# Retention gates of a decoder step: the first and the last eighth of a block in two halves of the token columns

## What is computed

```
q, k, v, gate = split(rms(x) @ w_in)          # 4 heads, dk 256, dv 512
o, s_fin      = retention(rope(q), rope(k), v, s0)
o             = (o - mean(o)) * rsqrt(var(o) + eps)
x            += (silu(gate) * o) @ w_out
s_new[b]      = g^4 * s0[b] + k_b^T v_b       # sampled sequences b = 0..7, state 256 x 512 for each head
```

## Time and profile before

| what | value |
|---|---|
| median of 3 runs | 1598.01 us (1594.16 to 1599.3) |
| the profiled execution, own time | 1594.63 us |
| its span in the profile | 1592.8 us |
| PE matmul busy | 1524.2 us, 96% |
| DVE busy | 949.0 us, 60% |
| ACT busy | 550.5 us, 35% |
| stage of the gates, head 0 | 92.09 to 126.52 us |

### The profile page before, as it was taken

How to read it: one execution, slowest core, us unless ns; L and a number is a source line. 1 busy time by engine, 2 the same in 40 slices (tenths; PEclk the granted TensorE clock), 3 DMA queues, 4 the chain that set the end, 5 groups by cost and what they waited for, 6 DMA issues and landing times.

```text
span 1592.8 us, 27562 instructions
## 1 busy us (share of the span) xinstructions
PE 1524.2 (96%) x11425; PEld 1427.9 (90%) x11425; DVE 949.0 (60%) x1286; ACT 550.5 (35%) x853; POOL 123.5 (8%) x111
## 2 busy tenths in 40 slices
PE   7999999999999899999999999988789999999997
PEld 7779978978987799999999999887689999999997
DVE  6547437435634688547736667564558854763763
ACT  5233133123223353322322354353435332322331
POOL 0000001001000120000000021341221000000001
PEclk9999999999999999999999999898899999999999
DMA  6346217216323223123222242111112213223123
GB/s 236 113 164 218 93 61 264 93 60 209 135 80 119 107 93 106 66 93 106 79 93 93 79 150 70 60 41 54 41 39 82 106 66 111 88 79 119 67 79 109
DMA packets 50152, 164.05 MB, mean 103 GB/s; under 512 B 5264, under 2 KB 6608, under 8 KB 50032
## 3 DMA queue, kind: packets, MB, share of 16 engines
q1 hardware_dynamic: 41888, 134.56, 24.3%
q0 software_dynamic: 6416, 24.93, 4.3%
q10 hardware_dynamic: 1760, 3.31, 0.6%
HBM read 141.35 MB, written 23.46 MB: 103 GB/s over the span
## 4 chain that ended last, share of the span: by engine, by line
PE 84%; DVE 8%; issue 3%; ACT 3%; POOL 1%; ACTq 0%; DVEq 0%; POOLq 0%
PE ps L466 48%; PE ps L1127 13%; PE ps L480 8%; DVE arena L1406 3%; PE ps L1316 3%; PE ps L984 2%; PE ps L993 1%; DVE w_lo L454 1%; PE ps L1015 1%; PE ps L1001 1%; PE ps L1279 1%; PE ps L1307 1%; DVE rstd L515 1%; PE ps L971 1%; PE ps L1030 1%
## 5 line engine op out<-in xcount | busy, mean ns | idle before, releaser
L449 ACT ACTIVATE w_hi<-w_raw 128x1024 fp32r<-128x1024 f32 x180 | 188.7, 1055 | 383.5 <-PE ps L466 233.0
L466 PE MATMUL ps<-xg_hi,w_hi 128*128 128x272 f32 x1280 | 268.6, 291 | 14.1 <-DVE xg_lo L1412 7.8
L466 PE MATMUL ps<-xg_hi,w_lo 128*128 128x272 f32 x1280 | 265.3, 289 | 0.0
L466 PE MATMUL ps<-xg_lo,w_hi 128*128 128x272 f32 x1280 | 264.9, 288 | 0.0
L454 DVE TENSOR_TENSOR w_lo<-w_raw,w_hi 128x1024 fp32r<-128x1024 f32 x172 | 212.9, 1241 | 70.8 <-ACT w_hi L449 69.6
L466 PEld LDWEIGHTS ps<-xg_hi,w_hi 128*128 128x128 f32 x1280 | 203.1, 189 | 23.6 <-issue 12.7
L466 PE MATMUL ps<-pr_hi,w_hi 128*128 128x272 f32 x992 | 210.4, 291 | 8.2 <-DVE pr_lo L1406 4.5
L466 PE MATMUL ps<-pr_hi,w_lo 128*128 128x272 f32 x992 | 209.7, 290 | 0.0
L466 PE MATMUL ps<-pr_lo,w_hi 128*128 128x272 f32 x992 | 208.9, 290 | 0.0
L466 PEld LDWEIGHTS ps<-xg_lo,w_hi 128*128 128x128 f32 x1280 | 202.0, 189 | 0.0
L466 PEld LDWEIGHTS ps<-xg_hi,w_lo 128*128 128x128 f32 x1280 | 200.8, 189 | 0.0
(11 more groups left out here) (247 smaller groups left out, 2639.4 us busy)
## 6 DMA issues: line engine op xcount, KB each, us to landing
w_raw<-in_w SPq DMA_DIRECT2D x180, 512.0 KB, 3.5
arena<-in_w SPq DMA_DIRECT2D x40, 512.0 KB, 4.5
arena<-in_state SPq DMA_DIRECT2D x32, 512.0 KB, 4.8
out_st_s<-arena POOLq DMA_DIRECT2D x32, 512.0 KB, 4.3
x<-in_x ACTq DMA_DIRECT2D x4, 544.0 KB, 6.0
out_y<-x POOLq DMA_DIRECT2D x8, 272.0 KB, 2.3
out_st_p<-arena SPq DMA_DIRECT2D x4, 512.0 KB, 2.8
arena<-in_dec POOLq DMA_DIRECT2D x4, 256.0 KB, 2.9
```

Source lines behind the costliest of these rows:

```text
L449: nc.scalar.activation(w_hi[:, n.c % 4, :], w_raw[:, n.c % 2, :], ACT.Copy).then_inc(w_hi_done, 1)
L466: last = pe.matmul(ps[:, 2 * bank_pair + s, 0:HT], w_of(w, k), xm[:, k, s * HT:(s + 1) * HT], start=(k == 0 and w == 0 and xi == 0), stop= ...
```

## The change

A gate block's eight steps over k are issued by hand. In step 0 and in step 7 the three matmuls of the first half of the columns (bank 0) come first and then the three of the second half (bank 1); steps 1 to 6 alternate between the halves as before. When the first half's last matmul is done it raises a new semaphore, `gate_half`; the second half's last raises `blocks` as before. DVE copies each half by itself, 128x272, the first after `gate_half`, the second after `blocks`, and each raises `gate_pre`, which so counts 8 for a head in place of 4. PE's next block waits for the first copy ahead of its first-half matmuls and for the second copy ahead of its second-half matmuls. ACT's Silu and the later waits ask for both halves.

```diff
-                    act.wait_ge(gate_pre, (one.times(4) + (g + 1)).v)
+                    act.wait_ge(gate_pre, (one.times(8) + (2 * g + 2)).v)
...
+                def gate_part(g, k, halves):
+                    for w, xs in ((w_hi, xg), (w_lo, xg[:1])):
+                        for xi, xm in enumerate(xs):
+                            for s in halves:
+                                last = pe.matmul(ps[:, 2 * GATE_PAIR + s, 0:HT], w[:, g, k * P:(k + 1) * P], xm[:, k, halves_of(s)],
+                                                 start=(k == 0 and w is w_hi and xi == 0), stop=(k == KT - 1 and w is w_lo))
+                    return last
+
+                def gate(g):
+
+                    for s in range(2):
+                        if g:
+                            pe.wait_ge(gate_pre, (one.times(8) + (2 * g - 1 + s)).v)
+                        gate_part(g, 0, (s,))
+                    for k in range(1, KT - 1):
+                        if k == KT // 2:
+                            beside_gate(g)
+                        gate_part(g, k, (0, 1))
+                    gate_part(g, KT - 1, (0,)).then_inc(gate_half, 1)
+                    gate_part(g, KT - 1, (1,)).then_inc(blocks, 1)
+
                 pe.wait_ge(vlo_done, (one + 1).v)
                 for g in range(4):
                     pe.wait_ge(w_lo_done, (n + (4 + g + 1)).v)
-                    if g:
-                        pe.wait_ge(gate_pre, (one.times(4) + g).v)
-                    product(pe, GATE_PAIR, w_tile(Index(g)), KT, xg,
-                            lambda k: beside_gate(g) if k == KT // 2 else None).then_inc(blocks, 1)
+                    gate(g)
                     state(2 * g + 1)
...
                     new_state(2 * g)
+                    dve.wait_ge(gate_half, (one.times(4) + (g + 1)).v)
+                    tt(gate_t[:, g, 0:HT], ps[:, 2 * GATE_PAIR, 0:HT], rstd[:, 0:HT], ALU.mult).then_inc(gate_pre, 1)
                     dve.wait_ge(blocks, (n + (4 + g + 1 + BIAS)).v)
-                    tt(two(gate_t[:, g, :]), pair(GATE_PAIR), two(rstd[:, :]), ALU.mult).then_inc(gate_pre, 1)
+                    tt(gate_t[:, g, HT:T], ps[:, 2 * GATE_PAIR + 1, 0:HT], rstd[:, HT:T], ALU.mult).then_inc(gate_pre, 1)
                     new_state(2 * g + 1)
```

More of the change, by code:

```diff
@@ L259, in build @@
         upd_done, s_new, s_out = sem("upd_done"), sem("s_new"), [sem(f"s_out{s}") for s in range(S_SLOTS)]
-        cross_evac, so_done, gate_pre, gate_act, gate_kept = sem("cross_evac"), sem("so_done"), sem("gate_pre"), sem("gate_act"), sem("gate_kept")
+        cross_evac, so_done, gate_half, gate_pre, gate_act, gate_kept = sem("cross_evac"), sem("so_done"), sem("gate_half"), sem("gate_pre"), sem("gate_act"), sem("gate_kept")
         so_centred, so_sqrt, so_normed, so_turned = sem("so_centred"), sem("so_sqrt"), sem("so_normed"), sem("so_turned")
@@ L1056, in before @@
                     if c == 2:
-                        pe.wait_ge(gate_pre, (one.times(4) + 4).v)
+                        pe.wait_ge(gate_pre, (one.times(8) + 8).v)
                 def beside(c, k):
```

## The result

The changed kernel takes 1587.63 us as the median of 12 runs, the kernel before 1596.15 us as the median of its 12 runs; the ratio is 0.9948, with a 95% interval of 0.994 to 0.9957. That is 8.3 us faster (6.9 to 9.6). The forecast was 1592.0, with a range of 1587.5 to 1597.0: the time lies at the fast end of it, next to the 1588.9 of the rival in which the loads keep up, to which I had given 12 in 100. The gain forecast was 4.5 us.

What follows compares the result with a forecast made beforehand. PE was taken to bound the kernel, stopping twelve times for gate copies. Heads 0 to 2 gave 2.5 us, head 3 2.0: 4.5 us off the 1596.5 mean, forecast 1592.0 us, range 1587.5 to 1597.0.

Steps and rivals of the forecast that it cites:

- the rival in which the loads keep up: State 7's load lands 2 us earlier as POOL's write gets shorter; all is won, 7.6 us, 1588.9 us; 12 in 100.
- The stops: PE's twelve waits for gate-block copies, 0.67 us each: 0.05 stays, 0.62 won at each, 7.4 us for twelve.
- The costs: Matmul order costs nothing; two half copies add 0.15 us of DVE per block, 2.4 us, hidden by DVE's wait.
- The stall at cross_of(1): In gate block 2, heads 0 to 2, PE newly waits about 1.0 us for state 7's load; none in head 3.
- if nothing else changes the load lands 0.2 earlier: State 7's load, heads 0 to 2: new_state(1) starts 0.2 us earlier, then write 5.8 us and load 4.5 us.
- the bounds: State 7's load landing: 0.3 us later if state 2's write takes transfer share, 0.5 earlier if the weight block clears.
- The term of 0.2 + 0.62: Gain in each of heads 0 to 2: 0.2 us from two stops ahead of cross_of(1), 0.62 from the third.
- signs of being wrong: PE still waiting for copies, no gap at cross_of(1), state 1's write far from 5.8 us, or single-half matmuls over 0.126 us apart.
- The sum: Heads 0 to 2 give 2.5 us, head 3 gives 2.0; together 4.5 us, ends 2.3 and 5.7.
- low end of 2.3: Smallest summed gain, if 0.13 us stays of each stop and state 7's load is 0.3 later.
- the last head's 0.15: In the last head, DVE's new_state(7) and what follows, for which PE waits, start some 0.15 us sooner.

Runs made afterwards that it cites:

- the order alone: Kernel before with only PE's first and last eighth done half by half; DVE copies the whole block, PE waits once: 1596.81 us, ratio 1.0005.
- the swap: SP issues the first weight block ahead of state 6's load: 1586.07 us on the changed kernel, 1594.19 us on the kernel before.
- the first eighth: Changed kernel, but the last eighth alternates as before and both copies start after the block's end; PE waits half by half: 1595.49 us, ratio 0.9989.
- POOL's delay: Changed kernel, but POOL zeroes 8 unused columns ahead of each write of state 1 (also called the late write): 1594.59 us, ratio 0.9988.

## Why the forecast was right, and where it was not

**The stops.** Right, and a little low. 0.05 of each was to stay; the rows after show 3.50 against 3.48, so 0.02, and 0.65 won where I had 0.62. In heads 1 to 3 that is 1.93 to 1.96 for three stops.

**The costs.** Right. The order costs nothing (run of the order alone: 1596.81 us, ratio 1.0005). Two copies of 442 ns take 0.82 us from start to end because the second overlaps the first, so DVE's extra is 0.1 us for a block, and PE nowhere waits for a gate's copy any more. DVE's idle time, 0.61 us ahead of the first copy of gate 0 in head 0, covered it; DVE's busy time went from 949.0 to 951.6 us, and that did not decide the time here.

**The stall at cross_of(1).** The place was right: it is the load of state 7, over new_state(1) and the write of state 1, that PE meets there once the stops are gone, and head 0 showed it in both profiles of the change. new_state(1) starts 0.50 us after the block's end, not 0.67, much as forecast. The step that failed is "if nothing else changes the load lands 0.2 earlier". The write did not keep its 5.8 us. It took 4.2, 4.1 and 4.1 in heads 0 to 2, 1.5 to 1.6 us less; with the earlier start that is more than the 1.24 by which PE now comes sooner. Counted from the start of the stage, the load landed 0.7, 1.9 and 1.6 us earlier, where the bounds went from 0.3 later to 0.5 earlier. In heads 1 and 2 it was there in time, and in head 0, where it took 5.5 us and not 4.5, the wait was 0.6 and not 1.0. The term of 0.2 + 0.62 for each of these heads measured 1.38, 1.95 and 1.93. Two of the prediction's own signs of being wrong were there: a write of state 1 far from 5.8 us, and no gap in two of the three heads. What makes the load of state 7 take 3.9 us in one head and 6.5 in another of these eleven profiles stays open.

That is the rival in which the loads keep up, and its reason, that POOL's write starts sooner and has the transfers to itself for longer, was tested: over the seven profiled kernels with SP's old order there are 21 writes of state 1 in heads 0 to 2. Where the write was issued 0.23 to 0.35 us ahead of state 6's load, ten times, it took 5.0 to 5.9 us; where 0.46 to 0.84, eleven times, 4.0 to 4.6. The weight block, the other load beside the write, does not sort them: it came 1.16 to 1.45 us behind the write in both groups. In the four kernels with the swap the lead is 1.5 to 1.8 and the write takes 3.5 to 4.0. One POOL instruction that cut the lead brought the long writes and the waits back in two heads, and the swap took the long writes away again. I had bounded this trip with the write's 5.8 as a fixed term, though head 3 stood there with 3.7, and I read that as a write with less company. It had the same company: state 6's load and the weight block were issued 0.97 and 1.45 us behind it, in head 0 0.31 and 1.45. The change's 0.2 us were just the difference that a lead of 0.3 lacked. Why the write's time falls by over a us between a lead of 0.35 and one of 0.46 was not tested.

**The sum.** 7.0 us by the traces' stretches, 8.3 (6.9 to 9.6) by the runs. That is nearly twice the 4.5 that was forecast, and close to the 7.6 of the rival. The time lay inside the range because the range reached to that rival; my own sum was off in all of heads 0 to 2. Its low end of 2.3 also leaves out the last head's 0.15, which the high end has; that decides nothing.

The spans of the two profiled executions differ by 8.7. Up to the first matmul of the first SwiGLU layer's mixed products the changed kernel is 5.9 us ahead: the 7.0, less 0.65 by which the gates of head 0 begin later and 0.44 behind the retention layer. From that matmul to the same one of the second SwiGLU layer, where the change does nothing, it is 633.0 us before and 630.1 after, but also 630.5 in the run of the order alone and 634.1 in that of the first eighth, which has the change's copies; the change, run again, has 632.6. The stretch holds the window attention, where PE stands still at times and the granted clock falls for a while: in the kernel before PE is busy for 0.93 of the four us from 992, and in the next four its clock is 0.50. Four us of it in the kernel before, by windows (window, length; busy us of PE, PEld, DVE, ACT and POOL, each with its number of instructions; PE's granted clock; DMA share and GB/s):

```profile
1008.00:1012.00 4.00, 4.00 (x42) 3.08 (x42) 1.90 (x8) 0.85 (x3) 1.49 (x1) 0.67 0.05 14
```

and four us of the changed kernel at about the same work (1002 here is some 1009 there):

```profile
1002.00:1006.00 4.00, 4.00 (x53) 3.65 (x50) 3.45 (x14) 0.46 (x2) 0.31 (x1) 1.00 0.25 70
```

In the first PE's granted clock was 0.50 in the last two us of the window, in the second it was 1.00 in all four. The same forty matmuls take 5.1 us from 1009.3 in the kernel before and 3.6 us from 1002.1 in the changed one. So 2.9 of the 8.7 us between the two profiles are not the change's, and how much of the 8.3 by the runs goes beyond the 7.0 that the traces place is not settled. This scatter is why the forecast's sum was rightly set against a mean and why the range had to be wide.

## What to carry to other kernels

An evacuation that an engine waits for on every block can be taken off its path without another buffer: finish one half a few matmuls early, copy it while the other half ends, and give each half its own signal; here that won 0.65 of the 0.67 us of each stop. Before counting such a gain, look what the engine meets next, and treat a transfer's time in that trip as a thing that the change may move: here a head start of 0.2 us was worth 1.6 us of a write, and with it over half of the gain in two heads of four. Where a trip has two transfers that start within some tenths of a us (here 0.23 to 0.35), put the order in by hand: the swap brought no time on the changed kernel that these runs can tell, but with it POOL's delay cost nothing (1587.37 us, and 1588.15 without the delay).

## What was not expected of the hardware

- A write of 512 KB to HBM took 5.0 to 5.9 us when a load of 512 KB was issued 0.23 to 0.35 us behind it, and 4.0 to 4.6 us when that load came 0.46 to 0.84 us behind it; no run had the load between 0.35 and 0.46 us behind.
- A GpSimd memset of 0.1 us ahead of a DMA issue put the issue off by 0.17 us, and that was enough to lose some 6 us of the 8.3 in the runs.
- Behind a stop of 2.56 us for a transfer, with the late write, PE's granted clock was 0.50 for 3.4 us, and the work behind the stop took 1.7 us longer.
- A second DVE copy behind a first one, each with its own wait, ended 0.82 us after the first began, though each is shown with 0.44.
